# A mixture-of-experts stage: gather and combination by rounded products with a 0/1 table

## Chip, cores, metric

One NeuronCore of a Trainium2 chip runs the whole program. The metric is the device time of one execution in microseconds (us).

## What is computed

A first transformer block (token mixer, then a mixture of experts) and a second block follow each other for 512 tokens of width 1024. The change concerns the experts:

```python
def expert_choice_ffn(h, w_router, w_gate, w_up, w_down):
    cap = CAPACITY_FACTOR * T // N_EXPERTS                      # 64 of 512 tokens, 16 experts
    aff = jax.nn.softmax((h @ w_router).astype(jnp.float32), axis=-1)
    gval, idx = lax.top_k(jnp.swapaxes(aff, 1, 2), cap)
    xe = jax.vmap(lambda hb, ib: hb[ib])(h, idx)
    hid = jax.nn.silu(jnp.einsum('becd,edf->becf', xe, w_gate)) * jnp.einsum('becd,edf->becf', xe, w_up)
    ye = jnp.einsum('becf,efd->becd', hid, w_down) * gval[..., None].astype(h.dtype)
    return jax.vmap(lambda yb, ib: jnp.zeros((T, D), yb.dtype).at[ib.reshape(-1)].add(yb.reshape(-1, D)))(ye, idx)

x = x + gt2 * expert_choice_ffn(h2, ...)
return rms_norm(x, final_norm)                                  # input of the second block
```

Each expert picks its 64 best tokens, computes a gated two-layer network on them, and adds the result, weighted, to those tokens' rows.

## The kernel before

All work of this stage is in `experts` (line 1832). It has two blocks of code, "route" and "experts", with a barrier of all engines at the end of each.

**Route.** For each of four tiles of 128 tokens, in the order `YORD`, TensorE ends the mixer's output product (`mixed`), VectorE adds it to `x1` and normalises into `h2` (`added`, `normed`; line 2009 is the last add), TensorE turns `h2` (line 1904), ScalarE evacuates (`turned`, line 1964), and the router's logits follow. VectorE takes the softmax (from line 2017 on), and eight rounds of the eight largest mark each expert's 64 tokens. Fifteen products with the identity (line 1943) go through TensorE meanwhile. `codet` then holds, for each token and expert, the token's place among the expert's 64, or 0. Comparing it with `iota` (1 to 64) gives `onehot`: a table of 0 and 1, tokens by places. Its part for the first two experts is built here (line 2044), that for the other fourteen at the start of the next block (line 2280).

**Experts.** The 16 experts go in 8 pairs: pair 0, a loop over pairs 1 to 6, pair 7 (`each_pair`). Two experts of 64 places fill 128 partitions. Weights come from HBM in chunks of 2048 KB, twelve a pair, into a ring of six slots; SyncE issues each load (line 1870) once the slot's last chunk has been used. TensorE's order in a pair is written out by hand in `pair`: gate-up of the first expert, combination of the pair before, gate-up of the second, gather for the pair after, turn of the hidden rows, turn of the weights, down product. The parts that matter here:

- Gather (line 2115): `xe = h2^T onehot`, 8 feature tiles by 4 token tiles, 32 full-precision products of 128 columns. The trace records a full-precision product as two passes.
- Own weights (line 2239): `onehot` times the affinities, turned by TensorE (line 2147) and copied to `wcur` (line 2249).
- Down product (line 2166): chunks 8 to 11 of the pair. VectorE scales the result by `GT2` into `ye` (line 2276).
- Combination (line 2141): 8 pieces (4 token tiles, 2 column halves) of 512 columns, `wcur^T ye`, in PSUM banks 0 and 1 in turn. VectorE adds each piece to `x1` (line 2256), which frees its bank (`cb_sb`).

After the last pair's combination the rows are normalised once more: squares on ScalarE (line 2220), a diagonal matrix of the deviations (line 2292), a product with it that also turns the rows (line 2196), and VectorE's evacuation with the final norm's weights (line 2297). SyncE issues the second block's first loads (lines 2094 to 2102) in the same queue, behind the experts' chunks.

Elsewhere in the kernel many products are already done with rounded operands: a value is split into `x_hi`, rounded to the type float32r, and the remainder `x_lo`, also of that type, and two or three products with rounded operands replace one in full precision. In the first and second block their names end in `_hi` and `_lo`.

Of the kernel before, what the change touches and what calls it, by code (L numbers as in the profile page):

```python
# [8 lines left out]
F32 = mybir.dt.float32  # L9
# [6 lines left out]
P = 128  # L16
# [54 lines left out]
def table1():  # L71
# [21 lines left out]
    t["iota"] = np.broadcast_to(np.arange(CAP) + 1, (P, CAP))  # L93
    t["fold"] = p % 32 == f[:, 0:16]
    return {k: np.asarray(v, np.float32) for k, v in t.items()}
# [1738 lines left out]
def experts(E, V):  # L1834
# [7 lines left out]
    x1, h2 = R.take(TT, D), R.take(TT, D)  # L1842
    H = Map(arena, V["ht_at"], V["ht_at"] + DK * NT * P)
    onehot = H.take(TT, NE * CAP)
    xe, hidT = H.take(DK, 2 * CAP), H.take(DK, 2 * CAP)
    wcur = R.take(512)
    h2T = yT
    ow = yT[:, 0, :].rearrange("p (t n) -> p t n", t=TT)
    ye, hs, hid = GT1, A2, SH2
    S = Map(arena, V["ht_at"], V["ht_at"] + DK * NT * P)  # L1850
    tmp = S.take(2, 512)
    sqs = S.take(D)
    S.at = V["ht_at"] + TT * NE * CAP
    affT, work, code = S.take(T), S.take(T), S.take(T)
    wr = sm[:, 400:656].rearrange("p (k n) -> p k n", k=DK)
# [5 lines left out]
    top8 = sm[:, 320:328]  # L1861

# [4 lines left out]
                         "ct_ps", "code_zero"))  # L1867

# [3 lines left out]
    with nc.Block("route") as block:  # L1872
# [77 lines left out]
        def _(act):  # L1950
# [19 lines left out]
            for n in range(3):  # L1970
                squares(n)
                deviation(n)
            turned(0)
            turned(1)
            logits(0)
# [5 lines left out]
            turned(3)  # L1981
            logits(3)
# [4 lines left out]
        def _(dve):  # L1987
# [55 lines left out]
            for t in range(TT):  # L2043
                nc.vector.tensor_tensor(heads(onehot[:, t, 0:2 * CAP], 2), over(C["iota"], 2), spread(codet[:, t, 0:2], CAP), ALU.is_equal)
# [8 lines left out]
    ow_sb, wt_ps, wc_sb = sem("ow_sb"), sem("wt_ps"), sem("wc_sb")  # L2053
    NP = NE // 2

# [18 lines left out]
    with nc.Block("experts") as block:  # L2074
        @block.sync
        def _(sp):
# [6 lines left out]
            with sp.Fori(1, NP) as i:  # L2083
# [6 lines left out]
                for s in range(RING):  # L2090
                    gate_up_used(i, s)
                    load_expert_chunk(sp, 2 * i + 1, s)
            sp.wait_ge(xe_ps, 2 * NP)
# [12 lines left out]
        def _(pe):  # L2106
# [64 lines left out]
            def pair(i, last=False):  # L2171
# [29 lines left out]
        def _(act):  # L2201
# [4 lines left out]
            def pair(i, last=False):  # L2206
# [9 lines left out]
                nc.scalar.activation(hidT[:, 4:8, :].rearrange("p k n -> p (k n)"), PS[:, 7, :], ACT.Copy).then_inc(hd_a, 1)  # L2216

            def squares(t):
                act.wait_ge(cb_sb, 8 * NP - 8 + 2 * t + 4)
# [16 lines left out]
        def _(dve):  # L2236
            def own_weights(i):
                for j in range(2):
                    last = nc.vector.tensor_tensor(ow[:, :, j * CAP:(j + 1) * CAP], onehot[:, :, bass.ds(2 * CAP * i + j * CAP, CAP)],
# [1808 lines left out]
```

## Time and profile before

| | us |
|---|---|
| median of 3 runs | 3082.7 (3081.36 to 3086.76) |
| the profiled execution | 3083.14 |
| its span, first to last instruction | 3081.3 |
| TensorE (PE) busy | 2980.7 (97%) |
| VectorE (DVE) busy | 1659.1 (54%) |
| ScalarE (ACT) busy | 1190.9 (39%) |
| mean granted TensorE clock | 0.991 of 2.4 GHz |

The rows of the section below come from this execution. Times are from the span's start. PEld is the load of a product's stationary operand, which overlaps PE. "arena" is the name under which the trace shows most of the kernel's memory. The DMA share is the mean busy share of the core's 16 DMA engines. In a timeline row the first number is the start, the second the length of the merged row, and the bracket the idle time before it and what ended it.

### The profile page before, as it was taken

The page shows a single profiled execution, that of the slowest core. Times are in us where ns is not written, and L with a number is a line of the kernel's source. Part 1 is how long each engine was busy: PE and PEld are TensorE (multiplying, and loading weights), DVE is VectorE, ACT ScalarE, POOL GpSimd, SP SyncE. Part 2 cuts the span into 40 slices and gives each one's busy share as a digit, 9 for nine tenths or more (in the row PEclk, how much of TensorE's full clock was granted, in tenths as well). Part 3 has the DMA queues.
Part 4 walks back from the last instruction along what each step waited for, and adds up shares of the span by engine and source line. Part 5 has one row for each costly group of instructions (what it writes and reads, how often), then busy time and mean ns, then how long its engine had stood idle before and what let it go on. Part 6 is the DMA issues. An engine that isn't in the chain of part 4 may idle for free.

```text
span 3081.3 us, 58082 instructions
## 1 busy us (share of the span) xinstructions
PE 2980.7 (97%) x24214; PEld 2523.1 (82%) x24214; DVE 1659.1 (54%) x2706; ACT 1190.9 (39%) x2273; POOL 963.2 (31%) x685
## 2 busy tenths in 40 slices
PE   7999899999999989999999999999999999999998
PEld 5678788544444449999998999999999999889996
DVE  4257755532212246847384558456676455477583
ACT  3154423110000035535524546346454443364453
POOL 1030367100000024233564432344332366343322
PEclk9999999989999999999999999999999999999999
DMA  7531100359999962322221122222332222113321
GB/s 305 222 129 55 70 3 3 139 214 427 429 429 429 429 264 75 110 83 103 81 99 55 56 97 101 92 103 76 109 110 76 97 83 83 56 69 110 110 78 53
DMA packets 38227, 440.07 MB, mean 143 GB/s; under 512 B 6104, under 2 KB 6744, under 8 KB 11994
## 3 DMA queue, kind: packets, MB, share of 16 engines
q1 hardware_dynamic: 36536, 435.29, 35.9%
q8 instruction: 181, 2.97, 0.4%
q10 hardware_dynamic: 1448, 1.31, 0.1%
q14 instruction: 62, 0.51, 0.1%
HBM read 433.69 MB, written 2.11 MB: 141 GB/s over the span
## 4 chain that ended last, share of the span: by engine, by line
PE 58%; DVE 2%; ACT 2%; issue 1%; POOL 0%; DVEq 0%; ACTq 0%
PE PS L3065 23%; PE PS L2933 23%; PE PS L2930 4%; PE PS L2944 2%; PE PS L3466 2%; PE PS L2521 1%; PE PS L3501 1%; PE PS L2527 1%; PE PS L3484 1%; ACT w_hi L2862 1%; DVE t_lo L3036 0%; ACT h_hi L2743 0%; PE PS L2534 0%; ACT low L2746 0%; PE PS L3461 0%
## 5 line engine op out<-in xcount | busy, mean ns | idle before, releaser
L2875 POOL TENSOR_TENSOR w_lo<-low,w_hi 128x512 fp32r<-128x512 f32 (+4 forms) x310 | 629.0, 2035 | 1522.0 <-ACT w_hi L2862 1517.1
L2862 ACT ACTIVATE w_hi<-low 128x512 fp32r<-128x512 f32 (+3 forms) x670 | 485.3, 743 | 475.4 <-PE PS L2933 290.0
L3065 PE MATMUL PS<-t_hi,w_hi 128*128 128x264 f32 (+1 forms) x1152 | 327.1, 284 | 7.8 <-ACT low L3139 7.8
L3065 PE MATMUL PS<-t_hi,w_lo 128*128 128x264 f32 (+1 forms) x1152 | 327.5, 284 | 0.0
L3065 PE MATMUL PS<-t_lo,w_hi 128*128 128x264 f32 (+1 forms) x1152 | 326.2, 283 | 0.0
L2880 DVE TENSOR_TENSOR w_lo<-low,w_hi 128x512 fp32r<-128x512 f32 x360 | 258.6, 735 | 31.8 <-ACT w_hi L2862 30.5
L3065 PE MATMUL PS<-h_hi,w_lo 128*128 128x264 f32 (+1 forms) x864 | 244.9, 283 | 0.0
L3065 PE MATMUL PS<-h_hi,w_hi 128*128 128x264 f32 (+1 forms) x864 | 244.5, 283 | 0.4 <-issue 0.4
L3065 PE MATMUL PS<-h_lo,w_hi 128*128 128x264 f32 (+1 forms) x864 | 244.8, 283 | 0.0
L2933 PE MATMUL PS<-g_hi,w_hi 128*128 128x264 f32 x1056 | 230.8, 286 | 1.2 <-DVE high L3327 1.2
L2933 PE MATMUL PS<-g_lo,w_hi 128*128 128x264 f32 x1056 | 228.6, 284 | 0.0
L3065 PEld LDWEIGHTS PS<-t_hi,w_hi 128*128 128x128 f32 x1152 | 217.3, 189 | 9.0 <-ACT low L3139 9.0
L2130 PE MATMUL PS<-arena 128*64 128x512 f32 x1024 | 223.1, 593 | 0.3 <-DMA arena<-wts_dram 0.3
L2933 PE MATMUL PS<-g_hi,w_lo 128*128 128x264 f32 x1008 | 218.6, 285 | 0.0
L3065 PEld LDWEIGHTS PS<-t_lo,w_hi 128*128 128x128 f32 x1152 | 217.3, 189 | 0.0
L3065 PEld LDWEIGHTS PS<-t_hi,w_lo 128*128 128x128 f32 x1152 | 216.8, 188 | 0.0
L3327 DVE SCALAR_TENSOR_TENSOR high<-PS,high 128x528 f32<-128x528 f32 (+1 forms) x84 | 58.8, 703 | 290.9 <-PE PS L2933 208.0
L2933 PE MATMUL PS<-h_hi,w_hi 128*128 128x264 f32 x928 | 202.3, 288 | 2.3 <-POOL w_lo L2875 2.1
L2933 PE MATMUL PS<-h_hi,w_lo 128*128 128x264 f32 x928 | 199.3, 285 | 0.0
L2933 PE MATMUL PS<-h_lo,w_hi 128*128 128x264 f32 x928 | 199.3, 285 | 0.0
L2130 PEld LDWEIGHTS PS<-arena 128*64 128x64 f32 x1024 | 79.0, 137 | 141.5 <-issue 139.6
L3139 ACT ACTIVATE low<-PS 128x264 f32<-128x264 f32 (+1 forms) x288 | 111.8, 388 | 189.0 <-PE PS L3065 182.4
(474 smaller groups left out, 6688.4 us busy)
## 6 DMA issues: line engine op xcount, KB each, us to landing
arena<-wts_dram SPq DMA_DIRECT2D x101, 2048.0 KB, 18.7
low<-wts_dram SPq DMA_DIRECT2D x77, 2048.0 KB, 7.8
arena<-wmod_dram SPq DMA_DIRECT2D x9, 2048.0 KB, 9.0
low<-wts_dram SPq DMA_DIRECT2D x12, 1536.0 KB, 6.4
arena<-na_bias_dram SPq DMA_DIRECT2D x16, 512.0 KB, 3.7
high<-tab_dram SPq DMA_DIRECT2D x1, 2225.0 KB, 25.6
arena<-x_cols_dram SPq DMA_DIRECT2D x1, 2048.0 KB, 8.7
arena<-x_dram SPq DMA_DIRECT2D x1, 2048.0 KB, 8.2
```

Source lines behind the costliest of these rows:

```text
L2130: last = nc.tensor.matmul(PS[a:b, 2 + 2 * j + half, :], xe[:, k, j * CAP:(j + 1) * CAP], w[:, x, k % 4, :], start=(k == 0), stop=(k == DK ...
L2521: mm = nc.tensor.matmul(PS[32 * j:32 * j + 32, b, at:at + QN], C[mean][:, 0:32], x[:, j * QN:(j + 1) * QN], start=first, stop=last)
L2862: nc.scalar.activation(hi, raw, ACT.Copy).then_inc(w_h.sem, 1)
L2875: nc.gpsimd.tensor_tensor(lo, raw, hi.bitcast(F32), ALU.subtract).then_inc(w_lp.sem, 1)
L2880: nc.vector.tensor_tensor(lo, raw, hi.bitcast(F32), ALU.subtract).then_inc(w_lv.sem, 1)
L2930: mm = nc.tensor.matmul(PS[:, b, :], w[wi], x[xi][:, NMETA:], **ends)
L2933: mm = nc.tensor.matmul(bank(b, h), w[wi], halves(x[xi])[:, h, :], **ends)
L2944: return nc.tensor.matmul(bank(2 * z, h), wts[z][wi][:, k * P:(k + 1) * P], part(x, h), start=first, stop=last)
L3065: last = nc.tensor.matmul(PS[:, b, 0:n], wt[wi][:, k, :], xs[xi], start=(i in (0, 1, 3) and k == 0 and j == 0), stop=(k == 3 and j == 2), ...
L3139: nc.scalar.activation(to, PS[:, 4 * (f % 2) + b, 0:width(fin)], ACT.Copy).then_inc(sv_sb.sem, 1)
L3327: nc.vector.scalar_tensor_tensor(toks(res[:, m, :], fin), sums(2 * (m % apart), fin), 0.5, toks(res[:, m, :], fin), ALU.mult, ALU.add).the ...
L3466: last = nc.tensor.matmul(PS[:, b, 0:256], (h_hi, h_lo)[xi][:, k, s:s + P], wt[wi].rearrange("p (k n) -> p k n", k=DK)[:, k, :], start=(k ...
```

## The change

- `h2` is split in "route" into `h2_hi` (ScalarE) and the remainder `h2_lo` (VectorE, in `h2`'s own place). The gather becomes 64 rounded products: `h2_hi` and `h2_lo`, each with a `onehot` of the rounded type; 0 and 1 are exact in it.
- `onehot` holds one pair only. The table for the pair after is built in each pair by VectorE (`next_onehot`), once the gather that reads it and the own weights are done. The build of fourteen experts ahead is gone, and TensorE waits for `oh_sb` before each gather.
- `wcur` becomes a table of 0 and 1 too (greater than 0), and the largest value of each turned row, `slot_aff`, is the place's affinity; it goes into the scaling of `ye`. `ye` is split into `ye_hi` (ScalarE) and `ye_lo` (VectorE), and a piece of the combination becomes two rounded products.
- The combination uses four banks (0, 1, 6, 7) instead of two, and the gather waits until all its pieces are added.
- Tables and tiles get other places in memory; `ident`, `iota` and `fold` come first in the table.

The core of the diff:

```diff
+    def split_high(act, n):
+        act.wait_ge(h2_done, n + 1)
+        nc.scalar.activation(h2_hi[:, YORD[n], :], h2[:, YORD[n], :], ACT.Copy).then_inc(hh, 1)
+
+    def split_low(dve, n):
+        dve.wait_ge(hh, n + 1)
+        dve.wait_ge(ht_ps, 2 * n + 2)
+        nc.vector.tensor_tensor(h2_lo[:, YORD[n], :], h2[:, YORD[n], :], h2_hi[:, YORD[n], :].bitcast(F32), ALU.subtract).then_inc(h_lo, 1)
...
             for n in range(3):
                 squares(n)
                 deviation(n)
+                if n == 1:
+                    split_high(act, 0)
+                    split_high(act, 1)
             turned(0)
             turned(1)
+            split_high(act, 2)
...
             turned(3)
+            split_high(act, 3)
             logits(3)
...
             for n in range(TT):
                 added(n)
                 normed(n)
+                if n == 2:
+                    split_low(dve, 0)
+                    split_low(dve, 1)
             nc.vector.memset(affT[0:NE, :], 1.0)
+            split_low(dve, 2)
+            split_low(dve, 3)
...
             def gather(i):
                 for k in range(DK):
-                    for t in range(TT):
-                        last = nc.tensor.matmul(PS[:, k // 4, (k % 4) * P:(k % 4 + 1) * P], h2[:, t, k * P:(k + 1) * P],
-                                                onehot[:, t, bass.ds(2 * CAP * i, 2 * CAP)], start=(t == 0), stop=(t == TT - 1))
+                    for x, part in enumerate((h2_hi, h2_lo)):
+                        for t in range(TT):
+                            last = nc.tensor.matmul(PS[:, k // 4, (k % 4) * P:(k % 4 + 1) * P], part[:, t, k * P:(k + 1) * P],
+                                                    onehot[:, t, :], start=(x == 0 and t == 0), stop=(x == 1 and t == TT - 1))
...
             def combine(i):
-                pe.wait_ge(ye_sb, 2 * i + 2)
+                pe.wait_ge(yl_sb, 2 * i + 2)
                 pe.wait_ge(wc_sb, i + 1)
                 for c in range(2 * TT):
                     t, half = divmod(c, 2)
                     pe.wait_ge(cb_sb, 8 * i + (c + 1))
-                    nc.tensor.matmul(PS[:, c % 2, :], wcur[:, t * P:(t + 1) * P], ye[:, half * 512:(half + 1) * 512],
-                                     start=True, stop=True).then_inc(cb_ps, 1)
+                    for x, part in enumerate((ye_hi, ye_lo)):
+                        last = nc.tensor.matmul(PS[:, CBANK[c % 4], :], wcur[:, t * P:(t + 1) * P], part[:, half * 512:(half + 1) * 512],
+                                                start=(x == 0), stop=(x == 1))
+                    last.then_inc(cb_ps, 1)
...
                 gate_up(i, 1)
+                if not isinstance(i, int) or i:
+                    pe.wait_ge(cb_sb, 8 * i + 4)
                 if not last:
-                    if not isinstance(i, int) or i:
-                        pe.wait_ge(cb_sb, 8 * i + 2)
-                    else:
-                        pe.wait_ge(oh_sb, 1)
+                    pe.wait_ge(oh_sb, i + 1)
                     gather(i + 1)
...
+                for half in range(2):
+                    act.wait_ge(ye_sb, 2 * i + (half + 1))
+                    lo, hi = half * 512, (half + 1) * 512
+                    nc.scalar.activation(ye_hi[:, lo:hi], ye[:, lo:hi], ACT.Copy).then_inc(yh_sb, 1)
...
             def turned_weights(i):
                 dve.wait_ge(wt_ps, i + 1)
-                nc.vector.tensor_copy(wcur, PS[:, 2, :]).then_inc(wc_sb, 1)
+                nc.vector.reduce_max(slot_aff, PS[:, 2, :], AX.X)
+                nc.vector.tensor_scalar(wcur, PS[:, 2, :], 0.0, None, ALU.is_gt).then_inc(wc_sb, 1)
+                nc.vector.drain()
+
+            def next_onehot(i):
+                dve.wait_ge(xe_ps, 2 * i + 2)
+                dve.wait_ge(ow_sb, i + 1)
+                for t in range(TT):
+                    last = nc.vector.tensor_tensor(heads(onehot[:, t, :], 2), over(C["iota"], 2), spread(codet[:, t, bass.ds(2 * i + 2, 2)], CAP),
+                                                   ALU.is_equal)
+                last.then_inc(oh_sb, 1)
...
                 own_weights(i)
+                if not last:
+                    next_onehot(i)
...
-                    nc.vector.tensor_tensor(ye[:, lo:hi], PS[:, 6 + half, :], GT2[:, lo:hi], ALU.mult).then_inc(ye_sb, 1)
-
-            nc.vector.drain().then_inc(cb_sb, 2)
-            for t in range(TT):
-                last = nc.vector.tensor_tensor(heads(onehot[:, t, 2 * CAP:], NE - 2), over(C["iota"], NE - 2), spread(codet[:, t, 2:], CAP),
-                                               ALU.is_equal)
-            last.then_inc(oh_sb, 1)
+                    nc.vector.scalar_tensor_tensor(ye[:, lo:hi], PS[:, 6 + half, :], slot_aff, GT2[:, lo:hi], ALU.mult, ALU.mult).then_inc(ye_sb, 1)
+                for half in range(2):
+                    dve.wait_ge(yh_sb, 2 * i + (half + 1))
+                    lo, hi = half * 512, (half + 1) * 512
+                    nc.vector.tensor_tensor(ye_lo[:, lo:hi], ye[:, lo:hi], ye_hi[:, lo:hi].bitcast(F32), ALU.subtract).then_inc(yl_sb, 1)
+
+            nc.vector.drain().then_inc(cb_sb, 4)
```

The order of instructions on TensorE in pair 7, where no register instructions stand between them. Line numbers of the changed kernel are its own; 2130 there is 2172 (gate-up), 2141 is 2184 (combination), 2155 is 2199 and 2147 is 2191 (turns), 2166 is 2210 (down). Before:

```order
L2130 MATMUL PS<-arena 64x512 x32
L2141 MATMUL PS<-arena 128x512 x8
L2130 MATMUL PS<-arena 64x512 x32
L2155 MATMUL PS<-arena 128x128 x8
L2147 MATMUL PS<-arena 128x128 x4
L2166 MATMUL PS<-arena 64x512 x32
L2141 MATMUL PS<-arena 128x512 x8
```

The 8 products of a combination stand in one row. In the changed kernel's loop over pairs a combination reads (its first rows):

```order
L2184 MATMUL PS<-ye_hi,wcur 128x512
L2184 MATMUL PS<-ye_lo,wcur 128x512
L2182 REGISTER_ALU
L2184 MATMUL PS<-ye_hi,wcur 128x512
L2184 MATMUL PS<-ye_lo,wcur 128x512
```

The combination keeps its place between the two gate-ups and has twice the products; nothing else changed places on TensorE.

VectorE between the first gather and the end of pair 0. Before:

```order
L2280 TENSOR_TENSOR arena<-arena 128x896 x4
L2245 COPY arena<-PS 128x512
L2239 TENSOR_TENSOR arena<-arena 128x4x64 x2
L2265 TENSOR_TENSOR arena<-arena,PS 64x512 x4
L2245 COPY arena<-PS 128x512
L2271 COPY arena<-PS 128x512
L2249 COPY arena<-PS 128x512
L2276 TENSOR_TENSOR arena<-PS,arena 128x512 x2
```

In the changed kernel:

```order
L2292 COPY arena<-PS 128x512
L2286 TENSOR_TENSOR arena<-onehot,arena 128x4x64 x2
L2304 TENSOR_TENSOR onehot<-arena 128x128 x4
L2324 TENSOR_TENSOR arena<-arena,PS 64x512 x4
L2292 COPY arena<-PS 128x512
L2330 COPY arena<-PS 128x512
L2296 TENSOR_REDUCE arena<-PS 128x1
L2297 TENSOR_SCALAR wcur<-PS 128x512
L2335 SCALAR_TENSOR_TENSOR ye<-PS,arena 128x512 x2
L2339 TENSOR_TENSOR ye_lo<-ye,ye_hi 128x512 x2
```

The wide build at the head is gone; four narrow builds (2304) stand behind the own weights, the copy of the turned weights became two passes (2296, 2297), and two subtractions (2339) end the pair.

## Rows read from the trace of the kernel before

**Rows 1.** Windows of the loop: length, busy time (instructions) of PE, PEld, DVE, ACT, POOL, clock, DMA share, GB/s.

```profile
675.00:1107.00 432.00, 429.84 (x2104) 193.19 (x2100) 89.35 (x138) 26.68 (x45) 0.00 (x0) 1.00 1.01 428
```

**Rows 2.** Timeline of PE, one pair from combination to combination.

```profile
781.26 7.88 PE L2141 MATMUL PS<-arena 128*128 128x512 f32 x16
789.07 13.95 PE L2130 MATMUL PS<-arena 128*64 128x512 f32 x64
802.95 7.41 PE L2115 MATMUL PS<-arena 128*128 x64
810.20 1.04 PE L2155 MATMUL PS<-arena 128*128 128x128 f32 x8
...
825.43 13.93 PE L2130 MATMUL PS<-arena 128*64 128x512 f32 x64
839.29 7.88 PE L2141 MATMUL PS<-arena 128*128 128x512 f32 x16
```

**Rows 3.** Issues of chunks: SyncE's timeline, then size and median us to landing, 620:700 and 820:1100.

```profile
662.96 424.43 SPq L1870 DMA_DIRECT2D arena<-wts_dram  x90
...
arena<-wts_dram SPq DMA_DIRECT2D x9, 2048.0 KB, 11.9
...
arena<-wts_dram SPq DMA_DIRECT2D x56, 2048.0 KB, 19.9
```

**Rows 4.** Timeline of PE, its waits for chunks and the last combination.

```profile
1068.40 3.65 PE L2130 MATMUL PS<-arena 128*64 128x512 f32 x16 [0.34 <-DMA arena<-wts_dram]
...
1107.90 3.65 PE L2166 MATMUL PS<-arena 128*64 128x512 f32 x16 [1.20 <-DMA arena<-wts_dram]
1112.35 7.70 PE L2141 MATMUL PS<-arena 128*128 128x512 f32 x16 [0.80 <-DVE arena L2276]
```

**Rows 5.** Timelines: rounded products of 248 and 512 columns; weight loads of 2-column passes.

```profile
2703.00 0.28 PE L2943 MATMUL PS<-h_hi,w_hi 128*128 128x248 f32 x1
...
2704.03 0.27 PE L2943 MATMUL PS<-h_hi,w_lo 128*128 128x248 f32 x1
...
2805.22 0.40 PE L2930 MATMUL PS<-g_hi,w_hi 128*128 128x512 f32 x1
...
2807.79 0.39 PE L2930 MATMUL PS<-g_hi,w_lo 128*128 128x512 f32 x1
...
30.76 0.97 PEld L416 LDWEIGHTS PS<-arena 128*128 128x128 f32 x8
```

**Rows 6.** Groups of instructions by line on DVE: the table's builds.

```profile
L2280 DVE TENSOR_TENSOR arena<-arena 128x896 f32<-128x896 f32 x4 | 4.1, 1086 | 0.4 <-PEq L1872 0.4
...
L2044 DVE TENSOR_TENSOR arena<-arena 128x128 f32<-128x128 f32 x4 | 0.9, 286 | 0.1
```

**Rows 7.** Timelines of ACT, DVE and PE, end of routing and first gather.

```profile
623.43 1.23 DVE L2009 TENSOR_TENSOR arena<-arena 128x1024 f32<-128x1024 f32 x1
...
626.72 0.60 ACT L1964 ACTIVATE arena<-PS 128x512 f32<-128x512 f32 x1 [0.26 <-PE PS L1904]
...
629.51 0.23 DVE L2017 TENSOR_REDUCE arena<-PS 128x4 f32<-128x64 f32 x1 [4.33 <-PE PS L1918]
...
650.33 9.01 PE L2115 MATMUL PS<-arena 128*128 128x128 f32 x64 [1.54 <-PEq L1872]
```

**Rows 8.** Timelines of DVE and SyncE after the last chunk.

```profile
1095.33 21.49 SPq L2099 DMA_DIRECT2D high<-ln_in_dram  x1
...
1111.60 0.69 DVE L2276 TENSOR_TENSOR arena<-PS,arena 128x512 f32<-128x512 f32 x1 [7.59 <-PE PS L2166]
...
1120.21 1.28 DVE L2256 TENSOR_TENSOR arena<-arena,PS 128x512 f32<-128x512 f32 x2
...
1123.97 1.29 DVE L2297 TENSOR_TENSOR high<-PS,high 128x512 f32<-128x512 f32 x2 [0.43 <-DMA high<-final_norm_dram]
```

**Rows 9.** Windows, columns as in rows 1: before the first gather, in it, a wait for a chunk.

```profile
648.00:651.00 3.00, 1.33 (x8) 1.12 (x9) 1.78 (x7) 0.00 (x0) 0.00 (x0) 0.93 0.00 0
651.00:654.00 3.00, 3.00 (x16) 3.00 (x16) 3.00 (x4) 0.00 (x0) 0.00 (x0) 0.50 0.00 0
...
1106.00:1109.00 3.00, 1.80 (x10) 0.49 (x8) 0.00 (x0) 0.00 (x0) 0.00 (x0) 1.00 0.97 413
```

More of the change, by code:

```diff
@@ L92, in table1 @@
     t["cos"], t["sin"] = cos.reshape(P, -1), sin.reshape(P, -1)
-    t["iota"] = np.broadcast_to(np.arange(CAP) + 1, (P, CAP))
-    t["fold"] = p % 32 == f[:, 0:16]
-    return {k: np.asarray(v, np.float32) for k, v in t.items()}
+    late = {"ident": t.pop("ident"), "iota": np.broadcast_to(np.arange(CAP) + 1, (P, CAP)), "fold": p % 32 == f[:, 0:16]}
+    return {k: np.asarray(v, np.float32) for k, v in (late | t).items()}
 def table2():
@@ L1841, in experts, with plain @@
     R = Map(arena, V["rest_at"], E["TOTAL"])
[L1842 to L1846, printed above, removed]
+    rounded, yT_at = V["rounded"], V["rest_at"] - DK * T
+    def plain(name, at, *shape):
+        n = int(np.prod(shape))
+        return nc.alloc_sbuf_tensor_at(name, [P, n], F32, offset=E["arena_at"] + 4 * at)[:, :].rearrange("p (a n) -> p a n", a=shape[0])
+    x1 = R.take(TT, D)
+    h2, h2_lo = plain("h2", R.at, TT, D), rounded("h2_lo", R.at, TT, D)
+    R.take(TT, D)
+    h2_at = -(-(RING * SLOT + sum(offsets(table1())[0]["fold"])) // 8) * 8
+    h2_hi = rounded("h2_hi", h2_at, TT, D)
+    ht_end = V["ht_at"] + DK * NT * P
+    S = Map(arena, -(-max(h2_at + TT * D, E["high_map"].base + offsets(table2())[1]) // 64) * 64, ht_end - DK * 2 * CAP)
+    tmp = S.take(2, 512)
+    sqs = S.take(D)
+    late_at = S.at
+    xe = Map(arena, late_at, S.end).take(DK, 2 * CAP)
+    hidT = Map(arena, S.end, ht_end).take(DK, 2 * CAP)
+    wcur = rounded("wcur", R.at, 1, 512)[:, 0, :]
+    R.take(512)
     h2T = yT
     ow = yT[:, 0, :].rearrange("p (t n) -> p t n", t=TT)
[L1849 to L1853, printed above, removed]
+    hs, hid = A2, SH2
+    ye, ye_lo = plain("ye", ht_end, 1, D)[:, 0, :], rounded("ye_lo", ht_end, 1, D)[:, 0, :]
+    ye_hi = rounded("ye_hi", yT_at + 2 * 512, 1, D)[:, 0, :]
     affT, work, code = S.take(T), S.take(T), S.take(T)
+    onehot = rounded("onehot", S.at, TT, 2 * CAP)
     wr = sm[:, 400:656].rearrange("p (k n) -> p k n", k=DK)
@@ L2043, in _ @@
             for t in range(TT):
-                nc.vector.tensor_tensor(heads(onehot[:, t, 0:2 * CAP], 2), over(C["iota"], 2), spread(codet[:, t, 0:2], CAP), ALU.is_equal)
+                nc.vector.tensor_tensor(heads(onehot[:, t, :], 2), over(C["iota"], 2), spread(codet[:, t, 0:2], CAP), ALU.is_equal)
     E["delta_sems"].release()
@@ L2053, in experts @@
     ow_sb, wt_ps, wc_sb = sem("ow_sb"), sem("wt_ps"), sem("wc_sb")
+    yh_sb, yl_sb = sem("yh_sb"), sem("yl_sb")
     NP = NE // 2
+    CBANK = (0, 1, 6, 7)
     LO, HI = (0, CAP), (CAP, 2 * CAP)
@@ L2082, in _, with load_pair @@
                 load_expert_chunk(sp, 1, s)
-            with sp.Fori(1, NP) as i:
+            def load_pair(i):
                 for s in range(RING):
@@ L2092, in _ @@
                     load_expert_chunk(sp, 2 * i + 1, s)
+            with sp.Fori(1, NP) as i:
+                load_pair(i)
             sp.wait_ge(xe_ps, 2 * NP)
@@ L2238, in own_weights @@
                 for j in range(2):
-                    last = nc.vector.tensor_tensor(ow[:, :, j * CAP:(j + 1) * CAP], onehot[:, :, bass.ds(2 * CAP * i + j * CAP, CAP)],
+                    last = nc.vector.tensor_tensor(ow[:, :, j * CAP:(j + 1) * CAP], onehot[:, :, j * CAP:(j + 1) * CAP].bitcast(F32),
                                                    aff[:, :, bass.ds(2 * i + j, 1)].to_broadcast([P, TT, CAP]), ALU.mult)
@@ L2255, in combined @@
                     x = x1[:, t, half * 512:(half + 1) * 512]
-                    nc.vector.tensor_tensor(x, x, PS[:, c % 2, :], ALU.add).then_inc(cb_sb, 1)
+                    nc.vector.tensor_tensor(x, x, PS[:, CBANK[c % 4], :], ALU.add).then_inc(cb_sb, 1)
             def pair(i, last=False):
                 own_weights(i)
+                if not last:
+                    next_onehot(i)
                 for j in range(2):
```

4 lines of the change are left out of this document (3 added, 1 removed).

## The prediction, written before the changed kernel ran

> **What bounds the kernel now.** I read the page first. Its slices show TensorE nearly full almost everywhere, and beside it a second full resource in the stretch from about 690 to 1080 us: the DMA engines. That stretch is the experts' loop, the only place that the change reworks. The windows confirm it: from 675 to 1107 us TensorE is busy 429.84 of 432.00 us while the DMA share is 1.01 at 428 GB/s [rows 1]. Two resources are full at once, so the question of this case is which one sets the end.
>
> TensorE's timeline gives the pair of experts as TensorE lives it: from one combination (line 2141) to the next 839.29 - 781.26 = 58.03 us. From start to next start it is made of 7.81 us for the combination, 13.88 for the second expert's gate-up, 7.25 for the gather (line 2115), 15.23 for the turns and the down product (lines 2155, 2147 and 2166; four chunks, so as long as a gate-up, and 1.4 of turns), and 13.86 for the next pair's first gate-up [rows 2]. No DMA wait stands in it.
>
> For the DMA engines a pair is 12 chunks of 2.097 MB. At 428 GB/s a chunk takes 4.90 us and a pair 58.8 us. So the transfers are already the slower of the two by 0.8 us a pair. That doesn't show for six pairs, because six chunks lie in the ring when the loop begins and the lead is eaten slowly: the time from a chunk's issue to its landing grows from a median of 11.9 in the first stretch to one of 19.9 us [rows 3], and TensorE meets its first wait for a chunk at 1068.40 (0.34 us), the next at 1107.90 (1.20 us), for the very last chunk [rows 4]. **In this kernel the last chunk of weights lands last; TensorE comes to it 1.2 us early.** The stream of 90 chunks begins when the first chunk of the ring is used up (issue at 662.96 [rows 3], 3.7 us after the first gather's end) and doesn't pause. Hence the end of the loop moves only with the start of the first gate-up and with what follows the last chunk.
>
> **The change, part by part.**
>
> *Combination.* Before: 8 full products of 512 columns, two banks, TensorE and VectorE in turns, 7.81 us [rows 2]. After: 16 rounded products. In the second block such products follow each other every (2807.79 - 2805.22) / 11 = 0.234 us [rows 5], so a piece takes 0.47 on TensorE; an operation on 512 columns takes VectorE 0.69 [rows 8]. With four banks TensorE does pieces 0 to 3 at once (1.9 us), then waits for the adds: piece 7 needs the add of piece 3, done about 0.6 + 4 x 0.69 = 3.4 us, and ends at 3.9. That is 3.9 us less a pair.
>
> *Gather.* Before: 32 full products of 128 columns, each two recorded passes, 7.25 us, 0.113 a pass. After: 64 rounded products of 128 columns, one pass each. The trace has no rounded product this narrow. Its nearest rows are 248 columns, 9 steps in 1.03 us, 0.114 each [rows 5]. Bounds: below, the slope between 248 and 512 columns (0.12 us for 264) takes 128 columns to 0.06; above, a rounded product as dear as a full one, 0.227. What keeps it from 0.06 is the weight load of 128 columns, one for each product: passes of only 2 columns with such a load still come every (0.97 - 0.19) / 7 = 0.111 us [rows 5]. I take 0.111: 64 x 0.111 = 7.1 us, as good as no change. The Trainium skill ("TensorE: Matmul & The Clock Gate", Back-to-back issue gap) gives about 81 ns for a stream of loads and 128-column matmuls; by it the gather would take 5.2 us, an estimate, and the sum would be some 2 us lower. No row here shows that pace with a full weight load.
>
> *TensorE's need per pair* becomes 58.03 - 3.9 - 0.15 = 54.0 us against 58.8 of transfers. It will wait about 4.8 us a pair for chunks, some 1.4 us before each of several (4.90 less 3.47 of use), from the second or third pair on. **Worth for the end: nothing.**
>
> *Table pair by pair, weights in 0/1 form, scaling.* VectorE loses one build of 4 x 1.09 us and gains per pair 4 builds of 128 columns, 0.29 each [rows 6], one more pass over the turned weights (0.69), and two subtractions (0.69 each): 3.2 us on an engine busy 89 of 432 us [rows 1]. ScalarE gains two copies of 512 columns, 0.60 each [rows 7]. The new chain (scaled output, rounded copy, remainder) is asked for only by the combination, a gate-up of 13.9 us later; the next table is asked for by the gather, later still; the two passes over the turned weights lie beside the down product of some 13.8 us. All hidden; were that cover gone, the chain would cost 1.4 us. It is gone once, at the last pair (below).
>
> *Routing, ahead of the loop.* Splitting the normalised rows costs ScalarE four copies of 128x1024 (two times 0.60 at most, I take 1.1) and VectorE four subtractions (1.23, as the add of that shape) [rows 7]. Three of each fall into waits for products. The last doesn't quite: ScalarE ends its last evacuation at 627.32, rounds until 628.4, and VectorE subtracts until about 629.75, where the maximum over the logits began at 629.51 after an idle of 4.33 us [rows 7]. Cost: +0.25 us on the path, between 0 and 1.
>
> *First gather.* From 650.33 to 659.34 it takes 9.0 us instead of 7.4, because it runs with the clock at 1.2 GHz to about 654 us [rows 7, 9]. After: 7.1 warm, plus 0 to 1.7 for the cold part; I take 8.0. So -0.9, between -5.1 (64 x 0.06 = 3.8) and 0 short of the dear case.
>
> *After the last chunk.* TensorE needs 3.65 us, then scaling ends at 1112.29 and the combination starts at 1112.35 [rows 4, 8]. The rounded copy and remainder put 1.4 us ahead of it; the first add then comes about 0.8 us after the first product (0.47 and the latency), near 1114.5, and eight at 0.69 end near 1120.0, some 1.5 us earlier than the 1121.5 of now [rows 8]. But neither decides: VectorE's evacuation of the features starts at 1123.97, after 0.43 us of waiting for the final norm's weights, a small DMA queued behind the same stream: the issue before it took 21.49 us in the queue's own row [rows 8]. It moves with the stream. Zero, with ScalarE's squares as next in line at about the same time.
>
> **Sum** against the profiled execution, 3083.14 us (span 3081.3 and 1.8 around it): +0.25 - 0.9 = -0.65 and all else 0. Its own time is 0.4 above the median of 3082.7, so the forecast is 3082.7 - 0.7 = **3082.0 us**. What a measurement of this kernel can tell from no change is 0.2%, 6.2 us.
>
> **The rivals.**
>
> *Narrow rounded products are dear* (slower). If the width of 128 columns costs a rounded product as much as a full one, 0.227 us, a gather takes 14.5 us and a pair 54.0 + 7.4 = 61.4 us, more than the 58.8 of transfers. TensorE then sets the end: 8 gathers x 7.25 more, 7 combinations x 3.9 less, less the 1.5 us of waits that stand there now [rows 4]: +29 us, 3112. It decides from (58.8 - 54.0) / 64 + 0.111 = 0.186 us a product. For: no row shows the width. Against: 248 columns show no such step, the pace is 0.114 us, near that of the weight load alone [rows 5]. 7 in 100.
>
> *The transfers give way* (faster). If the DMA engines carried more once asked for more, TensorE's 4.0 us a pair would count seven times: -29 us, 3054. Against: the share is 1.01 in the whole stretch and the backlog grows [rows 1, 3], so they were asked for more already. The Trainium skill ("DMA: Bandwidth & Descriptors", Where 436 GB/s comes from) puts the ceiling of the 16 ports at 435 GB/s, an estimate of 7 us less for 90 chunks than at the 428 that the row shows, so by the page this rival ends near 3075. 5 in 100.
>
> *The clock falls in the new waits.* After a stretch with TensorE busy 1.33 of 3 us the clock was at 1.2 GHz until 654; in one with 1.80, a wait for a chunk, it stayed at 2.4 [rows 9]. The new waits leave about 70% busy. If it falls, use of a chunk doubles to 6.9 us, TensorE has no waits, the clock returns, and 4.8 us of slack a pair absorb it. Only the end stays: last chunk 3.5 us and combination 1.5 later, +5, 3087. 8 in 100.
>
> *It does not do what it says*: the next table waits for the gather that reads the old one, and could come late. It is built under the down product and the next gate-up, with more than 20 us to spare. With other mishaps of placement 4 in 100, mostly slower.
>
> **How the numbers follow.** Forecast 76, dear products 7, transfers 5, clock 8, others 4. Faster by over 0.2%: the transfers and a tail of cheap first gather, 0.07. Slower: dear products, half of the clock case, most of the others, 0.14. Within: 0.79. Range: below, the cheap first gather (-5) and 1 us of scatter (the lowest run lies 1.3 below the median), 3076; above, the clock case and 3 us of scatter (the highest lies 4 above), 3090. The two far cases, 12 in 100, stay out.
>
> **What would show it.** Right: a gather of about 7 us, a combination near 4, waits of about 1.4 us for chunks in most pairs, a pair period of 58.8 us at the same 428 GB/s, and the last chunk landing within 2 us of 1107. Wrong: a pair period under 58 us with a higher rate; a gather over 12 us and no DMA waits; a granted clock of 0.5 inside the loop; a VectorE or ScalarE wait ahead of a combination.

## The result, and the profile after

The changed kernel takes 3089.6 us in the median (3087.7 to 3093.8, 9 runs), the kernel before 3084.3 (3081.4 to 3086.8, 9 runs): a ratio of 1.0021, 95% interval 1.0013 to 1.0030. The forecast was 3082.0; no change, within 0.2%, had 79 chances in 100, slower by more 14. The loss is 5.3 us. The profiled execution took 3089.25 us with a span of 3087.4, so it is 6.1 longer than that of before.

**The loop is as forecast.** Windows of the changed kernel, columns as in [rows 1]. The trace calls `h2_hi` and `h2_lo` h_hi and h_lo.

```profile
679.00:1111.00 432.00, 411.16 (x2104) 189.27 (x2100) 105.12 (x184) 36.24 (x60) 0.00 (x0) 1.00 1.01 428
```

TensorE is busy 411.16 of 432 us instead of 429.84, the DMA engines carry the same 428 GB/s, the granted clock is 1.00. Timeline of PE in one pair:

```profile
782.20 0.50 PE L2184 MATMUL PS<-ye_hi,wcur 128*128 128x512 f32 x1
...
832.45 3.65 PE L2172 MATMUL PS<-arena 128*64 128x512 f32 x16 [1.15 <-DMA arena<-wts_dram]
837.35 3.65 PE L2172 MATMUL PS<-arena 128*64 128x512 f32 x16 [1.24 <-DMA arena<-wts_dram]
840.93 0.50 PE L2184 MATMUL PS<-ye_hi,wcur 128*128 128x512 f32 x1
...
845.46 10.52 PE L2172 MATMUL PS<-arena 128*64 128x512 f32 x48
856.93 3.65 PE L2172 MATMUL PS<-arena 128*64 128x512 f32 x16 [0.95 <-DMA arena<-wts_dram]
860.51 0.66 PE L2157 MATMUL PS<-onehot,h_hi 128*128 128x128 f32 x4
861.01 0.61 PE L2157 MATMUL PS<-onehot,h_lo 128*128 128x128 f32 x4
...
867.71 1.06 PE L2199 MATMUL PS<-arena 128*128 128x128 f32 x8
```

The combination takes 845.46 - 840.93 = 4.5 us (7.81 in [rows 2]), the gather 867.71 - 860.51 = 7.2, so 0.112 a product, waits of about 1.2 us stand before chunks, and the combination comes 840.93 - 782.20 = 58.7 us after the one before it.

**The loss is ahead of the loop.** Timeline of PE, start and end of the first gather, then windows in it. PEq is TensorE's own sequencer. A stretch is called cold where the granted clock is 0.50 of 2.4 GHz, warm where it is 1.00.

```profile
649.28 0.63 PE L2157 MATMUL PS<-onehot,h_hi 128*128 128x128 f32 x4 [1.53 <-PEq L1897]
...
652.39 1.05 PE L2157 MATMUL PS<-onehot,h_lo 128*128 128x128 f32 x4
653.25 1.05 PE L2157 MATMUL PS<-onehot,h_hi 128*128 128x128 f32 x4
...
661.91 18.52 PE L2172 MATMUL PS<-arena 128*64 128x512 f32 x80
```

```profile
648.00:651.00 3.00, 1.72 (x14) 1.75 (x14) 0.90 (x5) 0.00 (x0) 0.00 (x0) 0.93 0.00 0
651.00:654.00 3.00, 3.00 (x16) 3.00 (x16) 0.00 (x0) 0.00 (x0) 0.00 (x0) 0.50 0.00 0
654.00:657.00 3.00, 3.00 (x16) 3.00 (x16) 1.36 (x3) 0.00 (x0) 0.00 (x0) 0.50 0.00 0
657.00:660.00 3.00, 3.00 (x16) 3.00 (x16) 0.00 (x0) 0.00 (x0) 0.00 (x0) 0.50 0.00 0
660.00:663.00 3.00, 3.00 (x14) 2.27 (x15) 0.90 (x4) 0.96 (x2) 0.00 (x0) 0.50 0.00 0
663.00:666.00 3.00, 3.00 (x14) 0.86 (x12) 0.00 (x0) 0.92 (x1) 0.00 (x0) 0.79 0.02 5
```

The gather starts 1 us earlier than in [rows 7] and ends 2.7 later: 12.6 us. Four products come every 0.86 us instead of 0.45. The clock falls to 0.50, as before, but where it was up again by 654, it now stays down until the gate-up has run for some us. SyncE's first issue and the last chunk move with it, by 3.8 and 3.7 us [rows 3, 4]. SyncE, then PE:

```profile
666.74 421.29 SPq L1895 DMA_DIRECT2D arena<-wts_dram  x90
```

```profile
1111.60 3.65 PE L2210 MATMUL PS<-arena 128*64 128x512 f32 x16 [1.25 <-DMA arena<-wts_dram]
1117.49 0.50 PE L2184 MATMUL PS<-ye_hi,wcur 128*128 128x512 f32 x1 [2.24 <-DVE ye_lo L2339]
1124.80 9.04 PE L2239 MATMUL PS<-arena 128*128 128x128 f32 x64 [1.78 <-DVE arena L2351]
1135.38 1.11 PE L2580 MATMUL PS<-high 128*32 128x132 f32 x32 [1.54 <-PEq L182]
```

The last chunk to the second block's start is 23.8 us (before 1130.22 - 1107.90 = 22.3). Line 2239 holds the products with the diagonal, called the feature products below. The kernel before, its feature products and the second block's start:

```profile
1120.35 7.45 PE L2196 MATMUL PS<-arena 128*128 128x128 f32 x64 [0.30 <-DVE arena L2292]
1130.22 1.11 PE L2521 MATMUL PS<-high 128*32 128x132 f32 x32 [2.41 <-PEq L183]
```

In the changed kernel the clock is down again there, windows:

```profile
1118.00:1121.00 3.00, 3.00 (x9) 2.30 (x9) 2.34 (x4) 1.15 (x2) 0.00 (x0) 0.53 1.00 426
1121.00:1124.00 3.00, 2.02 (x8) 1.33 (x6) 1.82 (x5) 2.46 (x4) 0.00 (x0) 0.90 1.00 421
1124.00:1127.00 3.00, 2.20 (x11) 2.20 (x12) 2.07 (x7) 2.45 (x6) 0.00 (x0) 0.67 0.52 123
```

**Theory:** one fall of the clock, at the head of the first gather, was there before too; the narrow rounded products do not end it, so it now lasts through the gather. **Rival:** the split of `h2`, the later start or VectorE's extra work cost the time, and the clock is a bystander.

### The profile page after: what moved, and what is told of

It reads as the page before. It is cut to its first block, busy times and chain, and to the rows that moved or that the text cites. A ratio compares the mean times of both kernels' runs of the same rounds, so it can differ in the third digit from the quotient of the medians.

```text
span 3087.4 us, 58180 instructions
## 1 busy us (share of the span) xinstructions
PE 2964.8 (96%) x24214; PEld 2525.4 (82%) x24214; DVE 1678.5 (54%) x2758; ACT 1207.6 (39%) x2293; POOL 963.8 (31%) x685
## 4 chain that ended last, share of the span: by engine, by line
PE 58%; DVE 2%; ACT 2%; issue 1%; POOL 0%; DVEq 0%; ACTq 0%
PE PS L3124 23%; PE PS L2992 23%; PE PS L2989 4%; PE PS L3003 2%; PE PS L3525 2%; PE PS L2580 1%; PE PS L3560 1%; PE PS L2586 1%; PE PS L3543 1%; ACT w_hi L2921 0%; ACT h_hi L2802 0%; PE PS L2593 0%; ACT low L2805 0%; PE PS L3520 0%; POOL w_lo L2934 0%
## 5 line engine op out<-in xcount | busy, mean ns | idle before, releaser
L3386 DVE SCALAR_TENSOR_TENSOR high<-PS,high 128x528 f32<-128x528 f32 (+1 forms) x84 | 58.8, 703 | 290.5 <-PE PS L2992 207.7
## 6 DMA issues: line engine op xcount, KB each, us to landing
arena<-wts_dram SPq DMA_DIRECT2D x101, 2048.0 KB, 22.3
```

Source lines behind the costliest of these rows:

```text
L3386: nc.vector.scalar_tensor_tensor(toks(res[:, m, :], fin), sums(2 * (m % apart), fin), 0.5, toks(res[:, m, :], fin), ALU.mult, ALU.add).the ...
```

## The experiments

Line numbers move by a few between kernels; the products are named by their operands. Experiments 1 to 3, 6 to 9, and 4 with 5 ran on three different chips, each with the kernel before beside them (medians 3082.9 of 21 runs, 3083.2 of 27, 3082.9 of 1); a ratio is to that kernel before.

**1. Longer filler ahead of the first gather** (`warm_gather`)

```diff
-            for _ in range(15):
+            for _ in range(17):
                 nc.tensor.matmul(PS[:, 7, :], C["ident"], h2T[:, 0, :], start=True, stop=True)
...
             last.then_inc(ct_ps, 1)
+            for _ in range(3):
+                nc.tensor.matmul(PS[:, 7, 0:256], C["ident"], h2T[:, 0, 0:256], start=True, stop=True)
```

> The changed kernel with TensorE kept busy up to the first gather: 17 instead of 15 products with the identity during the routing, and three more of 256 columns behind the turn of the codes. Theory (the first gather runs wholly at 1.2 GHz and delays the stream of weights): the clock is at 2.4 GHz in the first gather, which takes 7.1 us instead of 12.6; the first gate-up starts near 656.5 instead of 661.9, and so does the last chunk, near 1106 instead of 1111.6; the time falls by 4.5 to 6.5 us, to about 3084. Rival (the stream of weights is slower or later for another cause, such as the tables' new places or a fuller queue): the first gather is shorter but the last chunk still comes near 1111, and the time stays within 1.5 us.

3083.6 us against 3082.9 of the kernel before: ratio 0.9998 (0.9989 to 1.0007). The loss is gone, within what can be told. The first gate-up starts at 659.87 and not near 656.5 as expected, because the routing ended 3.3 us later in this execution; the gather's length is the expected one. Windows in its first gather (652.60 to 659.87, 7.27 us):

```profile
651.00:654.00 3.00, 2.70 (x20) 2.23 (x18) 1.12 (x5) 0.00 (x0) 0.00 (x0) 1.00 0.00 0
654.00:657.00 3.00, 3.00 (x30) 3.00 (x28) 0.60 (x1) 0.00 (x0) 0.00 (x0) 1.00 0.00 0
```

**2. The gather in full precision again** (`old_gather`): `h2` isn't split; all else of the change stays.

```diff
-                    for x, part in enumerate((h2_hi, h2_lo)):
...
+                    for t in range(TT):
+                        last = nc.tensor.matmul(PS[:, k // 4, (k % 4) * P:(k % 4 + 1) * P], h2[:, t, k * P:(k + 1) * P],
+                                                onehot[:, t, :].bitcast(F32), start=(t == 0), stop=(t == TT - 1))
```

> The changed kernel with the gather in full precision again (32 products of h2 with the 0/1 table) and without the split of h2; table pair by pair, combination in rounded halves, and four banks stay. Theory: the clock comes back within the first gather as before the change, so the first gate-up starts near 658 to 659 and the last chunk of weights is used near 1107 to 1108; the tail stays about 1.5 us longer than before the change; the time lies 3 to 5 us under the changed kernel's, near 3085.5. In the loop the pair period stays 58.8 us, since chunks are waited for. Rival (the combination or the tables are the cause): the time stays at the changed kernel's, 3089 to 3090.

3083.3 us, ratio 1.0002 (0.9993 to 1.0011). Its first gather, behind the same wait of 1.53 us, takes 659.96 - 652.64 = 7.3 us; the clock stayed at 1.00. The loss belongs to the rounded gather or its split of `h2`; experiment 1 keeps both and has no loss, so neither costs by itself while the clock is up. The time fell by some 6 us where 3 to 5 were expected, and the tail is 0.4 us longer than before the change, not 1.5. That the clock did not fall in this profile may be chance by itself (experiment 5 has more on that); the median of 11 runs is what counts.

**3. Which products bring the clock back?** The 15 identity products ahead of the gather become 64 rounded products of 128 columns (`fill_narrow`), or 60 of 512 (`fill_wide`). In both the new products also wait for `h2_hi`.

```diff
+            pe.wait_ge(hh, TT)
+            for n in range(64):
+                nc.tensor.matmul(PS[:, 7, 0:128], h2_hi[:, n % TT, 0:P], h2_hi[:, n % TT, 0:128], start=True, stop=True)
```

> The changed kernel with the 15 full-precision products of the routing replaced by 64 rounded products of 128 columns, which begin at 1.2 GHz as the others did. Only the clock is read. Theory (narrow rounded products, each with its weight load, do not bring the clock back): granted clock 0.50 through all 64, 0.213 us each, 13.7 us in all. Rival (the first gather's cold stretch was chance of timing): the clock returns to 1.00 within some 4 us and the rest runs at 0.112 us each, about 9 us in all.

> As the run with narrow fillers, but 60 rounded products of 512 columns. Only the clock is read. Theory (the width matters): starts at 0.50, returns to 1.00 within some 4 us, then 0.234 us each. Rival (the rounded type matters, not the width): 0.50 through all 60, 0.43 us each, 26 us, and everything behind them some 10 us later.

Windows, the narrow ones first, then the wide ones, both from a clock at 0.50:

```profile
630.00:633.00 3.00, 3.00 (x16) 3.00 (x16) 2.74 (x6) 0.00 (x0) 0.00 (x0) 0.50 0.00 0
633.00:636.00 3.00, 3.00 (x16) 3.00 (x16) 2.74 (x6) 0.00 (x0) 0.00 (x0) 0.50 0.00 0
636.00:639.00 3.00, 3.00 (x16) 3.00 (x16) 2.71 (x7) 0.00 (x0) 0.00 (x0) 0.50 0.01 3
```

```profile
630.00:633.00 3.00, 3.00 (x9) 2.42 (x8) 2.35 (x5) 0.00 (x0) 0.00 (x0) 0.50 0.00 0
633.00:636.00 3.00, 3.00 (x14) 2.40 (x14) 2.71 (x7) 0.00 (x0) 0.00 (x0) 0.97 0.00 0
636.00:639.00 3.00, 3.00 (x15) 2.49 (x14) 2.74 (x6) 0.00 (x0) 0.00 (x0) 1.00 0.00 0
```

TensorE is busy without a gap in both, yet the clock stays at 1.2 GHz for all 13.9 us of the narrow products, and through the gather behind them (13.8 us). Under the wide ones it is at 2.4 GHz from about 633; it then falls in the gather, which takes 12.2 us. The zeros of the table are not the reason: this filler multiplies `h2_hi` with itself, and narrow and wide fillers differ in the width alone. And the full-precision gather of before, under which the clock came back, has 16 recorded products and 16 loads in its cold window of 3 us as well [rows 9]. The times, 3087.8 and 3086.2 us, are single runs.

**4. Wide products in the middle of the cold gather** (`mid_wide3`)

```diff
                 for k in range(DK):
+                    if isinstance(i, int) and i == 0 and k == 2:
+                        for _ in range(3):
+                            nc.tensor.matmul(PS[:, 7, :], C["ident"], h2T[:, 0, :], start=True, stop=True)
```

> The changed kernel with three full-precision products of 512 columns put into the first gather behind its second slice (k = 2 of 8). Theory (the narrow rounded products do not bring the clock back, wide products do): the slices before them run at 0.213 us a product, the granted clock is back at 1.00 within about 3 us of their start, and the 48 narrow products behind them take some 0.112 us each, 5.4 us instead of 10.2; the three products cost 1.7 us each where the clock is down and 0.93 us where it is up. Rival (the clock comes back after a time of its own, whatever the products are, or falls again in narrow products): the products behind stay at 0.213 us.

Timeline of PE, then windows:

```profile
654.43 0.76 PE L2160 MATMUL PS<-onehot,h_lo 128*128 128x128 f32 x4
654.99 4.36 PE L2157 MATMUL PS<-arena 128*128 128x512 f32 x6
658.79 0.96 PE L2160 MATMUL PS<-onehot,h_hi 128*128 128x128 f32 x4
659.59 0.61 PE L2160 MATMUL PS<-onehot,h_lo 128*128 128x128 f32 x4
...
664.59 10.95 PE L2175 MATMUL PS<-arena 128*64 128x512 f32 x50
```

```profile
654.00:657.00 3.00, 3.00 (x13) 1.97 (x13) 0.00 (x0) 0.00 (x0) 0.00 (x0) 0.62 0.00 0
657.00:660.00 3.00, 3.00 (x13) 1.66 (x12) 0.00 (x0) 0.00 (x0) 0.00 (x0) 0.81 0.00 0
660.00:663.00 3.00, 3.00 (x29) 3.00 (x29) 1.36 (x3) 0.00 (x0) 0.00 (x0) 1.00 0.00 0
```

The fall came at about 654.7, behind most of the first two slices (so these were not at 0.213, a miss). The three wide products took 3.8 us and the clock came back under them; the 48 narrow ones behind took 5.8 us, 0.12 each, and kept it. A return after a time of its own would not care: in the changed kernel the clock stayed down for the 11 us that were left of the gather. The time, 3087.7 us, is of one run, with 3.8 us of filler in the path.

**5. What repeats** (`after_again3`, `before_again3`): both kernels once more, unchanged.

> The changed kernel once more, to see what of its profile repeats. Theory: the first gather is cold throughout again (12.6 us, granted clock 0.50), since it follows from the narrow products; the feature products may take 7.41 or 9.04 us, since the clock falls in the waits of the tail in some executions. Rival (the first profile was one chance): a first gather of under 10 us.

> The kernel before once more. Theory: its full-precision first gather starts behind the same wait and takes 7.3 to 9.0 us, as the clock falls in that wait or not; it is never cold throughout. Rival: a first gather of over 11 us here too, which would make the cold gather a matter of the wait and not of the products.

The changed kernel's first gather took 666.03 - 654.32 = 11.7 us with the clock at 0.50 from about 656.6, and its feature products 7.41 us. It was expected cold throughout, and was cold from 2.3 us behind its start. That of the kernel before took 7.3 us, clock 1.00. Behind this wait of 1.53 us the clock fell in one of three profiles with a full-precision gather ([rows 9]; not here and not in experiment 2) and in all four with a rounded one that began warm (the two of the changed kernel, `fill_wide`, `mid_wide3`). Whether the rounded products also make the fall likelier stays open. Single runs, 3092.3 and 3078.4 us.

**6. The kernel before with the filler behind the codes** (`before_warm`: the three products of 256 columns of experiment 1 alone).

> The kernel before, unchanged but for three full-precision products of 256 columns (0.45 us each) behind the turn of the codes, in the wait for the first one-hot table. Theory (the clock fell in that wait and cost the first gather 1.7 us of its 8.93): the first gather takes 7.2 to 7.4 us, and the median falls by 1 to 1.7 us. Rival (the clock's fall there comes and goes with its phase and is not caused by this wait): the gather's length does not change or the median stays within 0.5 us.

3081.4 us, ratio 0.9994 (0.9985 to 1.0003): 1.8 us less, not resolved. The first gather takes 7.3 us, as it did in `before_again3` without the filler, so nothing shows that the filler gains there.

**7. The tail** (`warm_both`: experiment 1, and two wide products in the 2.24 us before the last combination)

```diff
             each_pair(pe, pair)
+            for _ in range(2):
+                nc.tensor.matmul(PS[:, 4, :], hidT[:, 0, 0:P], hidT[:, 0:4, :].rearrange("p k n -> p (k n)"), start=True, stop=True)
             combine(NP - 1)
```

> The changed kernel with the longer clock filler ahead of the first gather (17 products instead of 15, and 3 of 256 columns behind the turn of the codes), and besides that two full-precision products of 512 columns (some 0.9 us each) in the wait of 2.24 us ahead of the last combination, on data that lies there. Theory (the second part of the loss is TensorE's clock, which falls after the longer wait for ye_lo): the clock stays at 1.00 through the last combination and the feature products, and the second block's start comes 1 to 2 us sooner after the last chunk than in the changed kernel; the median is 1 to 2 us below that of the kernel with the longer filler alone (3083.6), some 3082. Rival (the tail is held by VectorE's additions or by the wait itself, not by the clock): the granted clock rises but the median stays within 0.5 us of 3083.6.

3084.8 us, ratio 1.0004 (0.9995 to 1.0013). Nothing is gained over experiment 1 (0.9998), so the theory fails; the rival's half a us can't be told with this scatter. In the profile the 17 wide fillers began cold and ended late: the first gather starts 3.1 us after the codes are done (649.33 to 652.43), where the changed kernel has 2.25, and the stages below, counted from the gather, do not show this 0.9 us. In the tail the rival's account holds. The clock is 1.00 under the last combination (0.57 in `warm_gather`, 1115 to 1118), yet the last combination's start to the feature products takes 6.7 us here and 6.8 there. PE, `warm_gather` then `warm_both`:

```profile
1114.10 0.50 PE L2186 MATMUL PS<-ye_hi,wcur 128*128 128x512 f32 x1 [2.24 <-DVE ye_lo L2341]
1120.90 7.41 PE L2241 MATMUL PS<-arena 128*128 128x128 f32 x64 [1.25 <-DVE arena L2353]
```

```profile
1113.96 0.50 PE L2186 MATMUL PS<-ye_hi,wcur 128*128 128x512 f32 x1 [0.33 <-DVE ye_lo L2343]
1120.67 7.41 PE L2243 MATMUL PS<-arena 128*128 128x128 f32 x64 [2.67 <-DVE arena L2355]
```

What TensorE gains it waits for VectorE's diagonal (1.25, then 2.67 us). A cold feature product does cost: 9.04 instead of 7.41 us in all, in the first profile and in `light_pairs` below, in no other, and 1.1 us of it reaches the second block. A combination that is cold from its first or second product on costs 0.8 to 1.0 us (experiments 2 and 4).

**8. The first gather cut in two** (`early_first`: `warm_both`, and slices 5 to 7 behind the first chunk of the first gate-up)

```diff
-            gather(0)
+            gather(0, range(5))
...
+                        if isinstance(i, int) and i == 0 and j == 0 and half == 0 and k == 4:
+                            gather(0, range(5, DK))
```

> The same kernel with both fillers, and the first gather cut in two: slices k 0 to 4, then the first chunk of the first gate-up, then slices 5 to 7. Theory (what sets the end is when the first chunk is released, the stream of 90 chunks follows at its own pace): the first release comes 3 x 8 x 0.112 = 2.7 us sooner after the codes are turned, the last chunk is used 2.7 us sooner, the median is some 2.7 us below that of the kernel with both fillers, about 3079.5, and below the kernel before. Rival (the end is set by TensorE's own work in some pairs, or the queue cannot use the early release): less than 1 us comes through.

3081.9 us, ratio 0.9996 (0.9987 to 1.0006): no version beats the kernel before by what can be told. The median is 2.9 us below that of `warm_both`, near the 2.7 expected, but the two intervals overlap and the profile does not bear it out. The first issue is 655.75 - 647.43 = 8.3 us behind the gather's start instead of 11.0, but the second slot comes free 663.01 - 647.43 = 15.6 us behind it, where `warm_both` has 14.4, and the DMA engines idle between them. From start to second block 0.4 us is gained. Windows:

```profile
658.00:661.00 3.00, 2.22 (x13) 1.15 (x14) 0.90 (x4) 1.88 (x2) 0.00 (x0) 1.00 0.97 410
661.00:664.00 3.00, 3.00 (x16) 1.21 (x14) 0.36 (x1) 0.59 (x1) 0.00 (x0) 1.00 0.49 202
```

**9. Less work for TensorE** (`light_pairs`: `warm_both`, with the gathers of pairs 1 to 7 cut to the two products that close their banks, so their rows are not gathered)

> The kernel with both fillers, but the gathers of pairs 1 to 7 are cut from 64 products to the two that close their banks, so the rows of these pairs are not gathered (work left out). It takes some 7 us of TensorE's work from each of seven pairs. Theory (the transfers of the chunks set the pace of the loop): the pairs still follow each other every 58.7 to 59 us, and the time stays within 2 us of the kernel with both fillers. Rival (TensorE's work sets the pace): 7 x 7 = 49 us less, some 3033 us.

3081.6 us, one run, 3.2 below the median of `warm_both`: more than the 2 expected, far from the 49 of the rival; its first gather starts 2.2 us earlier than in the profile of `warm_both`, ahead of what was left out. Combinations follow each other every 952.75 - 894.02 = 58.7 us. PE:

```profile
894.02 0.50 PE L2190 MATMUL PS<-ye_hi,wcur 128*128 128x512 f32 x1
...
944.27 3.65 PE L2178 MATMUL PS<-arena 128*64 128x512 f32 x16 [1.24 <-DMA arena<-wts_dram]
949.16 3.65 PE L2178 MATMUL PS<-arena 128*64 128x512 f32 x16 [1.24 <-DMA arena<-wts_dram]
952.75 0.50 PE L2190 MATMUL PS<-ye_hi,wcur 128*128 128x512 f32 x1
```

Seven us less work in each of seven pairs gave nothing: the transfers set the pace.

**All profiles by stage**, us. The start of the first gather lies between 646.2 and 654.3 from run to run, mostly for reasons ahead of the change, so the stages are counted from it: to the first issue of a chunk (which takes in the gather), from there to the use of the last, from there to the second block's first product.

| kernel | first gather | to first issue | to last chunk | to second block | sum |
|---|---|---|---|---|---|
| before | 8.93 | 12.63 | 444.94 | 22.32 | 479.9 |
| before again | 7.32 | 11.01 | 444.61 | 22.21 | 477.8 |
| before, filler | 7.31 | 11.01 | 444.67 | 22.21 | 477.9 |
| after | 12.63 | 17.46 | 444.86 | 23.78 | 486.1 |
| after again | 11.71 | 17.50 | 444.79 | 22.06 | 484.4 |
| full-precision gather | 7.32 | 11.01 | 444.74 | 22.70 | 478.5 |
| filler (1) | 7.27 | 10.96 | 444.65 | 22.17 | 477.8 |
| both fillers | 7.26 | 10.96 | 444.67 | 22.08 | 477.7 |
| light pairs | 7.27 | 10.96 | 444.64 | 23.17 | 478.8 |
| narrow filler | 13.81 | 19.91 | 444.74 | 22.10 | 486.8 |
| wide filler | 12.17 | 17.48 | 444.69 | 22.10 | 484.3 |
| wide in the middle | 11.52 | 15.22 | 444.58 | 22.87 | 482.7 |
| gather in two | split | 8.32 | 446.88 | 22.09 | 477.3 |

The third column is the DMA stream: 444.6 to 444.9 us in all of them but the last row, whose stream has the hole. With the clock up the changed kernel needs what the kernel before needs, 477.8. Of the 8.3 us that its first profile has more, 5.4 are the cold gather, 1.1 the first chunk's use, cold too (4.83 us instead of 3.69), and 1.6 the tail (0.5 in the combination, 1.1 by the feature products). The first profile of before lies 2.1 us above 477.8 itself, 1.6 of it in its cold gather, so the two first profiles differ by 6.2.

## Why the prediction was wrong

- **Combination, gather in the loop, TensorE's need per pair, "worth for the end: nothing": right.** 4.5 us where 3.9 was forecast, 7.2 for 7.1, waits of about 1.2 for 1.4, a pair every 58.7 for 58.8 us, 428 GB/s. The sign "last chunk within 2 us of 1107" failed: it was used at 1111.60. `light_pairs` shows the cause and the table its size. The rounded product of 128 columns takes 0.112 us (0.111 forecast). The Trainium skill's 81 ns for a stream of loads and products of 128 columns ("TensorE: Matmul & The Clock Gate", Back-to-back issue gap) isn't seen, nor is the dear product.
- **"First gather ... I take 8.0": the step that failed.** The cold part was given at most 1.7 us, its size in [rows 9], as if the clock came back after the same time whatever runs. The trace showed only that it came back under full-precision products. Under rounded ones it did not: 12.6 and 11.7 us in the changed kernel, 13.8 and 12.2 behind the two other fillers. Against the profile of before the gather came out 3.7 us longer (12.63 for 8.93) where 0.9 less was forecast. The first chunk's use, 1.1 and 2.1 us more in the changed kernel's two profiles, since the clock was still down, wasn't in the sum at all. Experiment 1 takes both away and the loss with them; that is shown. Since the stream starts with this chunk, each us comes through, as the forecast's first part had said.
- **The rival "the clock falls in the new waits" was put in the wrong place.** It gave 3087, near the result, by a fall in the loop that costs at the last chunk (3.5 us) and the last combination (1.5). The clock stayed at 1.00 through the loop and the last chunk, and the combination lost 0.5; the fall that cost is one that was there before. The nearness is luck.
- **"After the last chunk ... Zero": right with the clock up** (22.1 to 22.2 us, before 22.2 to 22.3). But the change leaves TensorE a wait of 2.24 us and one of 1.2 to 2.7 where 0.80 and 0.30 stood, and in two profiles the clock was down under the feature products behind them, which lengthened the tail by 1.1 us (`light_pairs` 23.17, `warm_both` 22.08). In experiments 2 and 4 the feature products were warm, but the last combination took 0.8 to 1.0 us longer than in experiment 1, and the tail is 22.7 and 22.9.
- **"Routing ... +0.25": the size depends on the clock there.** From TensorE's first router products (line 1912, 1937 in the changed kernel) to VectorE's maximum over the logits it takes 10.94 us before and after where the stretch is cold (`before`, `warm_both`), and 9.46 before and 10.04 after where it is warm (`before_warm`, `early_first`): 0 to 0.6 us. The gather's start varies by 8 us for other reasons.
- **Chances.** Slower got 14 in 100, none of it from this stretch, though the range (3076 to 3090) just held the median of 3089.6. Its upper end came from the clock case and scatter, so that is luck too.

The Trainium skill says of the gate that it is set by how busy the array has been recently, and that the hardware doesn't count instructions ("TensorE: Matmul & The Clock Gate", What's actually happening). The traces bear out the fall after a pause. They don't bear out that a busy TensorE is enough to end it, as long as "busy" is what the profile shows: 3.00 of 3.00 us in every window that lies wholly in a cold rounded gather or in the narrow filler.

## What to carry to other kernels

A busy share of 100% does not say that the clock will come back. Before a stretch of full-precision products is made one of narrow rounded ones, look at the granted clock ahead of it; if there is a pause, close it with a few wide full-precision products (two more of 512 columns in the filler and three of 256 behind it took this kernel from 1.0021 to 0.9998 of the time before). And where a stream of transfers sets the pace of a loop, work taken from the loop is worth nothing, while a few cold us ahead of its first transfer come through whole.

## What was not expected of the hardware

- From a clock at 0.50, rounded products of 128 columns with a weight load each did not bring it back in 13.9 us, nor in the gather behind them; rounded ones of 512 columns did in about 3, full-precision ones of 128 by 654 [rows 9], those of 512 within the 3.8 us that three of them took. Why the two kinds of 128 columns differ stays open. Whether the width, the share of weight loads or the operands' type decides was not taken apart further.
- Once up, the clock stays up under the same narrow products: 7.2 us a gather in all pairs, and 5.8 us for the 48 of experiment 4. It wasn't seen to fall there without a pause shortly before; behind a pause it fell 1.3 to 2.3 us into the gather.
- In the cold a narrow rounded product takes 0.213 us, 1.9 times the 0.112 of the warm one.
- Releasing the first slot early is worth little alone: 2.7 us earlier brought 0.4 in the profile, since the second release came 1.2 us later.
